# One block for mixer, FFN and embedding, and an earlier staging order for the inputs of each down-projection group

## The reference

```
def trunk_layer(...):
    xn = rmsnorm(x, attn_norm_g)
    ...                                          # gated linear attention, differential attention
    h = x + mixer_output(gla_o, gg, diff_o, lam_init, w_out, gla_norm_g, diff_norm_g)
    hn = rmsnorm(h, ffn_norm_g)
    h = h + (jax.nn.silu(hn @ w_ffn_gate) * (hn @ w_ffn_up)) @ w_ffn_down
    gate = jax.nn.sigmoid(rmsnorm(h, ple_norm_g) @ w_ple_gate)
    h = h + gate * (p @ w_ple_proj)
```

## Time and profile before

| | us |
|---|---|
| median of 3 runs | 1916.06 (1913.25 to 1920.07) |
| profiled execution, device time | 1916.04 |
| its span (first to last instruction) | 1914.4 |
| TensorE busy in it | 1786.3 (93%) |
| VectorE busy | 1192.1 (62%) |
| ScalarE busy | 737.0 (39%) |
| mean granted TensorE clock | 0.971 of full speed |

### The profile page before, as it was taken

How to read it: one execution, slowest core, us unless ns; L and a number is a source line. 1 busy time by engine, 2 the same in 40 slices (tenths; PEclk the granted TensorE clock), 3 DMA queues, 4 the chain that set the end, 5 groups by cost and what they waited for, 6 DMA issues and landing times. The chain is left out here.

```text
span 1914.4 us, 35497 instructions
## 1 busy us (share of the span) xinstructions
PE 1786.3 (93%) x13062; PEld 1649.2 (86%) x13062; DVE 1192.1 (62%) x1945; ACT 737.0 (39%) x1417; POOL 337.0 (18%) x360
## 2 busy tenths in 40 slices
PE   6999999986999999987998999999999899998998
PEld 6999999884676666766898999999999898988897
DVE  4224733475777777764448776667766868689543
ACT  5114322653655656542324332223332334244320
POOL 1112321001233333342112111111111000000110
PEclk9999999898999999998999999999999999999999
DMA  4323541319999999974111222222222323232121
GB/s 161 104 79 80 150 126 56 91 51 288 320 339 358 342 363 354 337 238 145 45 33 56 68 73 86 68 72 75 69 80 94 123 87 116 73 104 74 56 69 47
DMA packets 232922, 265.72 MB, mean 139 GB/s; under 512 B 16162, under 2 KB 173428, under 8 KB 232756
## 3 DMA queue, kind: packets, MB, share of 16 engines
q1 hardware_dynamic: 211988, 195.36, 32.6%
q0 software_dynamic: 20768, 68.17, 10.6%
HBM read 229.79 MB, written 29.21 MB: 135 GB/s over the span
## 5 line engine op out<-in xcount | busy, mean ns | idle before, releaser
L2508 PE MATMUL psum<-x_second_hi,unit_hi 128*128 128x364 f32 x924 | 305.7, 331 | 13.6 <-DVE x_second_lo L2523 8.5
L2508 PE MATMUL psum<-x_second_hi,unit_lo 128*128 128x364 f32 x924 | 304.5, 330 | 0.0
L2508 PE MATMUL psum<-x_second_lo,unit_hi 128*128 128x364 f32 x924 | 304.4, 329 | 0.0
L150 PE MATMUL psum<-x_hi,w_hi 128*128 128x364 f32 x768 | 183.0, 347 | 9.1 <-DVE x_lo L2222 5.8
L1303 POOL DMA_DIRECT2D dec_v<-in_cache_v x256 | 138.0, 539 | 291.1 <-issue 285.5
L2508 PEld LDWEIGHTS psum<-x_second_hi,unit_hi 128*128 128x128 f32 x924 | 174.8, 189 | 16.2 <-issue 10.3
L2508 PE MATMUL psum<-x_first_hi,unit_hi 128*128 128x364 f32 x528 | 177.1, 335 | 9.5 <-DVE x_first_lo L2523 6.5
L2508 PE MATMUL psum<-x_first_hi,unit_lo 128*128 128x364 f32 x528 | 175.9, 333 | 0.0
L2508 PE MATMUL psum<-x_first_lo,unit_hi 128*128 128x364 f32 x528 | 175.8, 333 | 0.0
L2508 PEld LDWEIGHTS psum<-x_second_hi,unit_lo 128*128 128x128 f32 x924 | 174.7, 189 | 0.0
L2508 PEld LDWEIGHTS psum<-x_second_lo,unit_hi 128*128 128x128 f32 x924 | 174.7, 189 | 0.0
(11 more groups left out here) (310 smaller groups left out, 3321.5 us busy)
## 6 DMA issues: line engine op xcount, KB each, us to landing
dec_k<-in_cache_k SPq DMA_DIRECT2D x256, 256.0 KB, 5.4
dec_v<-in_cache_v POOLq DMA_DIRECT2D x256, 256.0 KB, 5.4
w_raw<-in_w_in SPq DMA_DIRECT2D x25, 512.0 KB, 3.9
scratch_z<-ffn_hidden SPq DMA_DIRECT2D x22, 546.0 KB, 2.8
w_raw<-in_w_ffn_gate SPq DMA_DIRECT2D x22, 512.0 KB, 3.7
w_raw<-in_w_ffn_up SPq DMA_DIRECT2D x22, 512.0 KB, 3.7
w_raw<-in_w_ffn_down SPq DMA_DIRECT2D x16, 512.0 KB, 3.9
feat_swap<-feat_n SPq DMA_DIRECT2D x32, 136.5 KB, 2.4
```

The source lines that it names most:

```text
L150: ins = pe.matmul(out[:, c, 0:SPAN], w(k), x(k)[:, c * SPAN:c * SPAN + SPAN], start=n == 0 and w is whi and x is xhi, stop=n == len(ks) - ...
L2508: ins = pe.matmul(bank[b], w[unit][:, j, :], x[slot][:, j, :], start=start and j == 0 and w is m.uhi and x is m.xhi7, stop=j == k - 1 and ...
```

## The change

The engine lists of `mixer`, `ffn` and `embedding` become functions that each stage returns, and `dense_stages` puts them one behind the other into a single block. The two all-engine barriers between the three are gone. In their place: TensorE waits for 7 evacuated mixer tiles before the FFN and for all 8 before P4 of tile 0; ScalarE and VectorE wait for all 8; SyncE waits for the last `unit_lo` and the sixth sum of squares before it loads `p`; ScalarE waits for the end of `ffn`'s evacuations before the high part of slice 6.

At a change of group, loads 2 and 4 go to the places of B21's and B13's high parts, after P3 and P4, ahead of load 1. On VectorE the low part of S3 moves behind X2, the low part of B23 ahead of X4, `common` of the tile before the group behind the low part of B21 in the first tile; the low parts of X3 and X2, and of X1 and X4, go ahead of the last two groups of evacuations of the tile before, that of B22 ahead of the first evacuations of the new tile. On ScalarE, B21's high part moves to the first tile, those of B13 and B23 go ahead of S1, and that of B22 goes behind the SiLU. Most lines of the diff are only shifted; without these it is:

```diff
-X_HI_B = {B11: 1, B21: 2, B13: 3, B23: 4, X3: 5, X2: 6, X1: 7, X4: 8, B22: 9}
+X_HI_B = {B11: 1, B13: 2, B23: 3, B21: 4, X3: 5, X2: 6, X1: 7, X4: 8, B22: 9}
...
 # ffn, SyncE
             if new:
-                    load_x(1, m.xlof[B21], t, 4, 1, 0)
-                    load_x(2, m.xhif[B13], t, 5, 0, 1)
-                    load_x(4, m.xhif[B23], t, 6, 1, 1)
+                load_x(2, m.xhif[B21], t, 4, 0, 1)
+                load_x(4, m.xhif[B13], t, 5, 1, 1)
+                load_x(1, m.xlof[B21], t, 4, 1, 0)
                 load_x(3, m.xlof[B13], t, 5, 0, 2)
                 load_x(5, m.xlof[B23], t, 6, 1, 2)
...
 # ffn, ScalarE
-                raw = {B13: 3, B23: 1, X3: 1, X2: 2, X1: 3, X4: 4}.get(slot)
+            raw = {B13: 1, B21: 3, X3: 1, X2: 2, X1: 3, X4: 4}.get(slot)
...
+        act.wait_ge(mixer_done, KT)
...
         for t in range(TILES):
-                if t:
-                    if first:
-                        z_hi(t, B23)
-                    unit_hi(act, m, s, t, S4)
-                    if first:
-                        copy_p1(t)
-                    if t <= GATE_TILES:
-                        silu(t - 1)
-                    if not first:
-                        copy_p1(t)
-                if first:
-                    for slot in (X3, X2, X1, X4, B22):
-                        z_hi(t, slot)
+            if first:
+                z_hi(t, B21)
+            if t:
+                unit_hi(act, m, s, t, S4)
+                copy_p1(t)
+            if first:
+                for slot in (X3, X2, X1, X4):
+                    z_hi(t, slot)
+            if 1 <= t <= GATE_TILES:
+                silu(t - 1)
+            if first:
+                z_hi(t, B22)
...
             unit_hi(act, m, s, t + 1, A21)
-                if new:
-                    z_hi(t + 1, B21)
             unit_hi(act, m, s, t + 1, S3)
             unit_hi(act, m, s, t + 1, S2)
-                unit_hi(act, m, s, t + 1, S1)
             if new:
                 z_hi(t + 1, B13)
+                z_hi(t + 1, B23)
+            unit_hi(act, m, s, t + 1, S1)
             unit_hi(act, m, s, t + 1, A22)
...
 # ffn, TensorE
+        pe.wait_ge(mixer_done, KT - 1)
...
                 if t == 0:
+                    if n == 4:
+                        pe.wait_ge(mixer_done, KT)
...
 # ffn, VectorE
-                first, second = m.xhif[B13][:, 0:n, :], m.xhif[B23][:, 0:n, :]
+            first, second = m.xhif[B21][:, 0:n, :], m.xhif[B13][:, 0:n, :]
...
+        dve.wait_ge(mixer_done, KT)
...
             if first:
-                    z_lo(t, B23)
                 z_lo(t, B21)
+                common(t - 1)
                 for unit in (S2, S1, A22):
                     unit_lo(dve, m, s, t, unit)
+                z_lo(t, X3)
+                z_lo(t, X2)
                 bottom_right(t - 1)
+                z_lo(t, X1)
+                z_lo(t, X4)
                 bottom_left(t - 1)
             if t:
                 top_right(t - 1)
                 unit_lo(dve, m, s, t, S4)
                 if t <= GATE_TILES and not first:
                     hidden(t - 1)
+            if first:
+                z_lo(t, B22)
             third(t)
             top_left(t)
             if first:
-                    z_lo(t, X3)
-                    third_of_second(t)
-                    z_lo(t, X2)
-                    z_lo(t, X1)
-                    common(t)
-                    z_lo(t, X4)
-                    z_lo(t, B22)
                 for unit in (A11, A12, A21):
                     unit_lo(dve, m, s, t + 1, unit)
-                    bottom_right(t)
+                third_of_second(t)
+                common(t)
                 if t == GATE_TILES:
                     hidden(t - 1)
                 unit_sums(dve, m, s, t + 1)
                 unit_lo(dve, m, s, t + 1, S3)
+                bottom_right(t)
                 bottom_left(t)
...
             if new:
                 z_raw(t + 1, X3)
                 z_raw(t + 1, X2)
+                unit_lo(dve, m, s, t + 1, S3)
                 z_raw(t + 1, X1)
                 z_lo(t + 1, B11)
-                    z_raw(t + 1, X4)
                 z_lo(t + 1, B13)
+                z_lo(t + 1, B23)
+                z_raw(t + 1, X4)
                 continue
...
 # embedding, SyncE, then ScalarE
+        sp.wait_ge(done["w_lo"], NUNIT * TILES)
+        sp.wait_ge(new["new_h_sum"], 6)
...
             for n in range(3, KT):
+            if n == 6:
+                act.wait_ge(done["evacuated"], NEV * TILES)
+                act.wait_ge(done["h_added"], 3 * (TILES - GATE_TILES))
                 new_hi(act, m, new, n)
...
+def dense_stages(nc, stages):
+    with nc.Block() as block:
+        @block.sync
+        def _(sp):
+            for sync, _, _, _, _ in stages:
+                sync(sp)
...
-        for phases in ((input_projection, gla), (attention, mixer, ffn, embedding)):
+        for phases in ((input_projection, gla), (attention, dense_stages)):
```

More of the change, by code:

```diff
@@ new lines, in gpsimd, with scale @@
+    def gpsimd(gp):
+        def scale(u, gains, done):
+            gp.tensor_tensor(m.raw[:, u], m.raw[:, u], gains.unsqueeze(2).broadcast_to([P, KT, P]), ALU.mult
+                             ).then_inc(done, 1)
+        with gp.Fori(1, 4) as i:
+            for u in range(2):
+                gp.wait_ge(w_in[u], i * 16 + 16)
+                scale(u, m.mg, s["w_scaled"])
+        for u in range(2):
+            gp.wait_ge(ffn_w_in[u], 16)
+            scale(u, gain(m, "ffn"), ffn_w_scaled)
@@ L2705, in _ @@
                 third_of_second(t)
[L2706 to L2708 removed]
                 common(t)
[L2710 to L2719 removed]
+                if t == GATE_TILES:
+                    hidden(t - 1)
@@ L2729, in _ @@
-            top_right(last)
-            new_lo(dve, m, s, 0)
+                for unit in (S2, S1, A22):
+                    unit_lo(dve, m, s, t + 1, unit)
+                continue
+            if FIRST_OF[-1] < t:
+                for n in pair_of(t - 1):
+                    new_sum(dve, m, s, n)
+            if t < last:
+                unit_sums(dve, m, s, t + 1)
+                unit_lo(dve, m, s, t + 1, A11)
+                unit_lo(dve, m, s, t + 1, A12)
+            third_of_second(t)
@@ new lines, in vector @@
+            if t < last:
+                unit_lo(dve, m, s, t + 1, A21)
+            if new:
+                z_raw(t + 1, X3)
+                z_raw(t + 1, X2)
+                unit_lo(dve, m, s, t + 1, S3)
+                z_raw(t + 1, X1)
+                z_lo(t + 1, B11)
+                z_lo(t + 1, B13)
+                z_lo(t + 1, B23)
+                z_raw(t + 1, X4)
+                continue
+            if t < last:
+                unit_lo(dve, m, s, t + 1, S3)
+            common(t)
@@ L2793, in _ @@
-            with gp.Fori(0, 3) as i:
-                for u in range(2):
-                    scale(i, u)
+            for _, gpsimd, _, _, _ in stages:
+                gpsimd(gp)
         @block.scalar
         def _(act):
-            def hi(n, u):
-                act.wait_ge(s["w_scaled"], n + 1)
-                if not (isinstance(n, int) and n < 2):
-                    act.wait_ge(s["gate_done"], n - 1)
-                act.activation(m.whi[:, u], m.raw[:, u], ACT.Copy).then_inc(s["w_hi"], 1)
@@ L2818, in _ @@
[L2818 to L2829 removed]
+            for _, _, scalar, _, _ in stages:
+                scalar(act)
         @block.tensor
@@ L2874, in proj @@
-            def proj(w, n, k):
-                return w[:, k, n, :]
-            pe.wait_ge(new["new_h_lo"], 1)
-            tile(0, 0, [(k, [lambda k=k: pe.wait_ge(new["new_h_lo"], k + 2)] * (k + 1 < KT)
-                         + [lambda k=k: turn_p(k - 1)] * (1 <= k <= PT)) for k in range(KT)])
-            for n in range(1, KT):
-                tile(n, n % 2, turn(n - 1, 1 - n % 2))
-            for _, parts in turn(7, 1):
-                for part in parts:
-                    part()
+            for _, _, _, tensor, _ in stages:
+                tensor(pe)
```

1353 lines of the change are left out of this document (671 added, 682 removed).

## The result

| | before | after |
|---|---|---|
| median, us (lowest to highest) | 1914.05 (1910.73 to 1920.07), 5 runs | 1895.40 (1893.92 to 1901.09), 5 runs |
| span of the profiled execution, us | 1914.4 | 1893.4 |
| mean granted TensorE clock | 0.971 | 0.977 |

The direction was right and the size was not. Of the 7.4 us between 1895.4 and the forecast of 1902.8, 2.0 are the kernel before, whose median of five runs is 1914.05 and not 1916.06; the other 5.4 are the change.

A forecast was written before the change was run, and what follows sets the result against it. TensorE, busy 93% of 1914.4 us, was taken as the bound; only its idle time and clock could give time back. Gains 2.4 + 4.0 + 3.8 + 2.6 + 0.4 = 13.2 gave 1902.8 us, range 1898 to 1910.

The forecast's parts named there:

- the step on the first barrier: Mixer/FFN barrier: the chain moves by 2.4 us, TensorE waits longer in tile 1; gain 2.4, not 3.0 + 2.9.
- 2.9 later less what P7 would have idled: First barrier's lower bound: if the clock halves at P2, P7 comes 2.9 later less 1.6 idle; gain 1.2 us.
- Loads: Change to group 1: load 4, issued after P4, takes 5.6 us, so X3's sum starts 2.1 us sooner.
- loads bound: Rival, chance 0.12: the queue is full from 1484, load 4 lands no sooner, groups 1 and 2 gain 2.1 less each: 1906.9.
- loads in order: Assumption named with the first barrier's bounds for the range's lower end, 1898 us.
- Groups: The three FFN group changes gain 4.0, 3.8 and 2.6 us; in group 1 P0, P3, P10 idle 1.1, 1.5, 1.9.
- Second barrier: FFN/embedding barrier: VectorE's unbroken chain starts sooner, gain 0.4 of 3.56 us; the 2.94 wait on p_lo grows by about 3.
- counted at full clock: Residual idle times were assumed to be followed by full clock, as after 1.06, 1.17 and 2.22 us.
- the clock rival: Chance 0.15: half clock follows some idle times of 1.1 to 1.9 us; three stretches take 6.5 of the gain: 1909.
- the barriers pay in full: Rival, chance 0.05: VectorE's chains behind the barriers don't bind, so 3.0 + 2.9 and 3.6 instead of 2.8: 1896.
- ScalarE blocks: Rival, chance 0.03, slower: B23's high part waits for load 5 ahead of other high parts; load at 1504.3 gives 1922.

The follow-up runs named there:

- minus_copy: The kernel after, with ScalarE's older order in gate tiles, SiLU ahead of the bank 0 copy: 1902.05 us, ratio 0.9940 to before.
- one_block_only: The kernel before, with its three stages in a single block and waits on producers, no order changed: 1912.72 us, ratio 0.9996 to before.
- both_orders: The kernel after with the edits of both embedding_order and scalar_order: 1888.23 us, ratio 0.9863 to before.
- embedding_order: The kernel after, with VectorE and ScalarE reordered in the embedding's first tile, weights' low parts last: 1892.70 us, ratio 0.9887 to before.
- scalar_order: The kernel after, ScalarE's B22 high part ahead of SiLU in group 1, bank 0 copy earlier in groups' second tiles: 1891.39 us, ratio 0.9888 to before.
- minus_one_block: The kernel after, with three blocks and their two barriers again, all orders as changed: 1896.95 us, ratio 0.9911 to before.
- groups_only: The kernel before with the new order at the three group changes alone, three blocks, SiLU ahead of the copy: 1903.92 us, ratio 0.9945 to before.
- copy_only: The kernel before, with only ScalarE's bank 0 copy moved ahead of the SiLU in all gate tiles: 1907.93 us, ratio 0.9970 to before.

## Why the prediction was wrong, and where it was right

**The step that failed** is the one on the first barrier, in its last part: from the row scale on, ScalarE's "work is unbroken to the SiLU and the bank 0 copy for which P3 of tile 1 waits 5.05 us", so "the whole chain moves by 2.4; TensorE just waits longer in tile 1". This took the order of SiLU and copy from the kernel before. The diff reverses it, in the list that I read for the change of a group only, and the sum has no term for it. The row was in front of me, 5.05 us with ScalarE's copy as releaser, and so was the half clock behind it. The windows view of before puts the clock after that wait beside the two that the prediction priced:

```profile
1039.83:1045.15 5.32, 5.32 (x18) 5.32 (x18) 2.72 (x5) 1.10 (x2) 1.90 (x1) 0.50 0.37 137
```

With 17 matmuls started in it in 5.32 us instead of 2.83, it cost 2.5 beside the 5.05: 7.5 in all, of the 7.7 in the table, and 6.7 and 6.8 by the two experiments. The prediction named its own test, "wrong would be the step on the first barrier if tile 1's wait shrinks", and it went to nothing. Adding this one term gives 13.2 + 6.7 = 19.9 for 18.7 measured.

**First barrier, the rest.** Right: 2.3 for 2.4. P2 idles 1.86 for 1.7. The part by which VectorE gains more than the barrier shows: GpSimd's scaling of a weight starts at 994.53, and the two `unit_lo` that took 2.56 under it take 1.29. Timelines of POOL and DVE after:

```profile
994.53 1.90 POOL L2382 TENSOR_TENSOR w_raw<-w_raw,gains 128x1024 f32<-128x1024 f32 x1 [13.79 <-DMA w_raw<-in_w_ffn_gate]
...
1003.67 1.29 DVE L1910 TENSOR_TENSOR unit_lo<-unit_sums,unit_hi 128x512 fp32r<-128x512 f32 x2
```

P7's idle time was to be 1.6. It is 1.48 in minus_copy, one_block_only and both_orders, 1.49 in embedding_order, and absent in after and scalar_order, where the granted clock fell to 0.50 at P2 and P7's input was ready by the time it came: the bound "2.9 later less what P7 would have idled" worked as written, with 1.6 in place of 2.9, and so costs almost nothing. The 2.9 is what the 20 matmuls from 1001.40 on lost in before: 6.20 us for 20 x 0.166.

**Loads.** Near in this profile, in part by luck. X3's sum starts 7.45 us after P3's end in tile 21, forecast 7.6, which is 5.45 after P4's end, when load 4 is issued:

```profile
1478.48 1.68 DVE L2519 TENSOR_TENSOR x_second_lo_raw<-x_first_hi_raw,x_second_hi_raw 128x1456 f32<-128x1456 f32 x1 [2.13 <-DMA x_first_hi_raw<-scratch_z]
```

The rival *loads bound* would have kept it at 9.7. But the same load in the same order took 4.7, 4.9, 5.4, 5.9, 6.1, 6.1 and 6.3 us at group 1 in the seven profiles with the new order (minus_one_block, minus_copy, after, groups_only, embedding_order, both_orders, scalar_order), and 4.2 to 4.9 at group 2. P0's idle time follows it: 0.32, 0.52, 1.01, 1.55, 1.77, 1.74 and 1.98 at group 1. So 5.6 and "1.1" lay within a spread of 1.7 us, and one profile could not have confirmed them. The lower end of the range, 1898, has "loads in order" in it, an earlier landing of load 4. That term was an assumption of mine that no run shows; in its place the runs showed those landings, 4.7 to 6.3 us at group 1, on both sides of the 5.6, and 4.2 to 4.9 at group 2, all below it. What makes the load's time vary stays open.

**Groups.** The sum is right to 0.1, with two errors that cancel. In group 1 the idle times at P0, P3 and P10 are 1.01, 1.24, 1.48 for 1.1, 1.5, 1.9, and tile 22 ends 5.05 sooner for 4.65. (The 1.5 was a slip: 1504.35 and twice 0.5 are 1505.35, which gives 1.25.) But I let tile 23 wait 0.65 at P5 for VectorE, and it waits 1.91 at P3 for the copy of bank 0. ScalarE's list has the copy behind high parts of `unit_sums`, and these end late because VectorE makes the sums late. Timeline of ACT after:

```profile
1516.05 1.75 ACT L1904 ACTIVATE unit_hi<-unit_sums 128x512 fp32r<-128x512 f32 x3 [7.22 <-DVE unit_sums L1924]
...
1518.74 0.45 ACT L2412 ACTIVATE rstd_and_products<-psum 128x364 f32<-128x364 f32 x1
```

I had followed VectorE's lateness along VectorE's own queue into the next tile and not onto ScalarE's. Hence 3.1 for 4.0. Group 2 gives 4.7 for 3.8; in it, P0 idles 0.40 for 1.1, because load 4 took 4.8 us there and not 5.6, and the clock, which before had halved over ten matmuls there, stayed whole. Group 3: 2.7 for 2.6.

**Second barrier.** Half right. VectorE's chain is unbroken and starts sooner as forecast: the low part of `p` is begun 15.33 us after the FFN's end for 15.74 before, 0.41 for 0.4. The wait grows from 2.94 by 2.93, "longer by about 3". But I stopped the account at that row. The longer wait was followed by the lower clock, which 2.94 was not: from these transposes to the second group of matmuls that reads a low part of `h` it takes 5.4 us (1754.29 to 1759.67) for 2.9 before (1777.24 to 1780.13), and to tile 1 15.9 for 13.2, 2.6 lost. So tile 1 of the embedding starts 2.2 later, of which 0.7 came back behind it. The term was +0.4, it is -1.5. I had said that residual idle times are "counted at full clock"; for those of about 1 to 2 us that was a choice with a rival beside it, for one of 5.9, longer than the 5.05 and the 3.01, behind which the clock was 0.50 in before, it had no row on its side.

**Clock.** The windows of after: behind the 1.86, behind the 5.87, and behind the 1.91 (the column ahead of the last two is the granted clock):

```profile
1002.20:1005.60 3.40, 3.40 (x11) 3.40 (x12) 3.37 (x5) 2.48 (x5) 0.00 (x0) 0.51 0.00 0
1755.03:1759.60 4.57, 4.57 (x18) 4.49 (x17) 3.05 (x3) 3.08 (x4) 0.00 (x0) 0.50 0.03 9
1519.25:1522.50 3.25, 3.25 (x20) 3.25 (x21) 3.21 (x6) 1.15 (x2) 0.00 (x0) 1.00 0.37 110
```

The prediction's test for the clock rival was a window of 0.50 behind a wait below 2 us, and there is one. It did not decide: the half clock cost 1.6 there, which P7 gave back, and at the three groups the waits of 0.3 to 1.9 were all followed by full clock. In the FFN before, stretches at half clock began at 1001.40, 1039.83, 1499.63, 1516.24 and 1598.06, together 9.8 us lost; in the FFN after there is the one at 1002.20. With shorter idle times there were fewer of them, and the mean clock rose from 0.971 to 0.977.

In weighing that rival I also misread the kernel before. I wrote that 2.66 was the shortest idle time that halved the clock and that 1.06 to 2.22 did not. A wait of 2.16 us stood at 1515.31, and the stretch from 1516.24 on followed it. The timeline of PE and the windows of before:

```profile
1515.31 0.41 PE L2508 MATMUL psum<-x_second_hi,unit_hi 128*128 128x364 f32 x1 [2.16 <-DVE x_second_lo L2523]
```

```profile
1515.31:1519.57 4.26, 4.26 (x16) 4.26 (x17) 3.47 (x3) 4.26 (x6) 0.00 (x0) 0.60 0.01 4
```

With it the rival deserved more than 0.15 for P2, the one wait of that size.

**The rivals.** *Loads bound* and *the barriers pay in full* did not happen: the single block without the rest gives 1.6 (interval of the ratio 0.9987 to 1.0005), not the 9.5 (3.0 + 2.9 + 3.6) of that rival. *ScalarE blocks* did not either: ScalarE waits 3.40 and 0.57 us for raw B13 and raw B23, but it has caught up before the copy for P3, where it idles 3.48 us for VectorE; tile 22 waits at P0, P3 and P10 alone. The change that was forecast is the one that took place, plus a move that was not costed.

## What to carry to other kernels

Cost a reordering by the diff's lists, engine by engine and for every kind of tile that runs them, not only for the tile that the change is about: two lines that swap inside a shared loop body were worth 6.7 of 18.7 us here, more than the removal of two barriers, which gave nothing measurable. For every idle time in the profile ask whether any line of the diff touches its releaser's queue. And where a barrier goes, work out the wait that takes its place together with what follows it: the last wait grew from 2.94 to 5.87, and half clock followed it in the profile. Last, set a forecast of a few tenths of a microsecond against more than one profile: the load that it hung on here took 4.7 to 6.3 us.

## What was not expected of the hardware

The same wait, of the same length and at the same place, is followed by half clock in some executions and by full clock in others. Behind 1.86 us before P2 of tile 0 the granted clock is 0.51 in after and 1.00 in one_block_only:

```profile
1000.50:1004.00 3.50, 3.50 (x21) 3.50 (x22) 3.48 (x5) 2.47 (x5) 0.00 (x0) 1.00 0.00 0
```

Behind 1.91 before P3 of tile 23 it is 1.00 in after and 0.51 in embedding_order, whose program is the same up to there:

```profile
1523.13:1526.50 3.37, 3.37 (x13) 3.37 (x13) 3.34 (x7) 1.26 (x2) 0.00 (x0) 0.51 0.10 29
```

Behind the second barrier's 3.56 us it is 1.00 throughout in copy_only and fell to 0.50 in the three other kernels that have that barrier.

The ten profiles together show what followed each idle time of the FFN and of the embedding's first two tiles. None of up to 1.77 us was followed by a fall of the clock to 0.50. Of those from 1.85 to 3.56, 28 of 44 were, the shortest of them 1.86. All seven from 4.34 to 5.87 were. An unbroken stretch lost 1.4 to 3.0 us. So by these counts an idle time cut from 5 to 1 us gives back more than 4, one cut from 3 to 2 perhaps nothing more than the 1, and a forecast should carry both cases for what lies between. What decides there in a given execution stays open.
